# Two transformer blocks on one core: when groups are evicted, a stage's end barrier, the order of two loads and the place of a hosted sum

## The reference

```
mod = silu(c) @ w_mod + b_mod                     # shift, scale, gate rows
p   = modulate(rmsnorm(x), sh1, sc1) @ w_in       # mq mk mv mo mg | dq dk dv
h   = mlstm(forward) + flip(mlstm(backward))
y   = concat([rmsnorm(h) * sigmoid(mo), diff_heads]) @ w_out
x   = x + ga1 * rmsnorm(y, g_post_mix)
```

## Time and profile before

| | |
|---|---|
| time, median of 3 runs | 2983.63 us (2981.06 to 2983.66) |
| profiled execution | 2983.62 us, its span 2981.8 us |
| mean TensorE clock | 0.989 of full |
| busy TensorE / VectorE / ScalarE / GpSimd | 2867.1 / 2049.0 / 1243.8 / 145.2 us |
| HBM read | 572.21 MB |

### The profile page before, as it was taken

How to read it: one execution, slowest core, us unless ns; L and a number is a source line. 1 busy time by engine, 2 the same in 40 slices (tenths; PEclk the granted TensorE clock), 3 DMA queues, 4 the chain that set the end, 5 groups by cost and what they waited for, 6 DMA issues and landing times.

```text
span 2981.8 us, 38127 instructions
## 1 busy us (share of the span) xinstructions
PE 2867.1 (96%) x14307; PEld 2344.2 (79%) x14307; DVE 2049.0 (69%) x2919; ACT 1243.8 (42%) x2120; POOL 145.2 (5%) x225
## 2 busy tenths in 40 slices
PE   6999999998999999999999999999999999999998
PEld 2587667988778888887887888887878887888886
DVE  3368745837778889997895848873457686775466
ACT  3322525517345455454344332324445224445353
POOL 1100000001010000000000100000001001001000
PEclk9999999999999999999999999999999999999999
DMA  9877044841768777787886545772214564775334
GB/s 364 306 267 241 25 136 154 279 168 36 274 203 266 253 255 251 250 265 250 283 289 206 184 131 167 239 228 69 75 57 153 204 212 130 239 267 156 105 126 146
DMA packets 282822, 589.44 MB, mean 198 GB/s; under 512 B 31073, under 2 KB 64073, under 8 KB 278928
## 3 DMA queue, kind: packets, MB, share of 16 engines
q1 hardware_dynamic: 272240, 546.64, 56.0%
q0 software_dynamic: 10000, 39.72, 3.8%
q10 hardware_dynamic: 400, 0.66, 0.1%
HBM read 572.21 MB, written 14.72 MB: 197 GB/s over the span
## 4 chain that ended last, share of the span: by engine, by line
PE 75%; DVE 7%; ACT 3%; issue 2%; DMA 1%; POOL 0%; DVEq 0%; ACTq 0%; POOLq 0%
PE bank L3299 19%; PE bank L3301 19%; PE bank L3300 19%; PE bank L3309 2%; PE bank L3311 2%; PE bank L3310 2%; PE bank L1423 2%; DVE acc L739 2%; DVE w_lo L3236 1%; PE bank L1414 1%; ACT w_hi L3206 1%; PE bank L2453 1%; PE bank L883 1%; PE bank L1126 0%; PE bank L999 0%
## 5 line engine op out<-in xcount | busy, mean ns | idle before, releaser
L3236 DVE TENSOR_TENSOR w_lo<-raw,w_hi 128x1024 fp32r<-128x1024 f32 (+2 forms) x668 | 785.4, 1187 | 435.5 <-ACT w_hi L3206 428.0
L3206 ACT ACTIVATE w_hi<-raw 128x1024 fp32r<-128x1024 f32 (+2 forms) x668 | 679.6, 1031 | 913.9 <-PE bank L3301 639.1
L739 DVE SCALAR_TENSOR_TENSOR acc<-raw,sc_t,acc 128x1024 f32<-128x1024 f32 x480 | 601.3, 1280 | 23.6 <-DMA acc<-in_b_ada 18.7
L3299 PE MATMUL bank<-w_hi,l_hT_hi 128*128 128x512 f32 (+1 forms) x1056 | 390.2, 370 | 7.0 <-DVE w_lo L3236 4.8
L3301 PE MATMUL bank<-w_hi,l_hT_lo 128*128 128x512 f32 (+1 forms) x1056 | 387.6, 367 | 0.0
L3300 PE MATMUL bank<-w_lo,l_hT_hi 128*128 128x512 f32 (+1 forms) x1056 | 387.4, 367 | 0.0
L3299 PE MATMUL bank<-w_hi,f_hT_hi 128*128 128x512 f32 x704 | 278.1, 395 | 1.4 <-DVE mod L787 1.1
L3301 PE MATMUL bank<-w_hi,f_hT_lo 128*128 128x512 f32 x704 | 275.0, 391 | 0.0
L3300 PE MATMUL bank<-w_lo,f_hT_hi 128*128 128x512 f32 x704 | 274.8, 390 | 0.0
L3299 PEld LDWEIGHTS bank<-w_hi,l_hT_hi 128*128 128x128 f32 x1056 | 198.8, 188 | 43.7 <-DVE w_lo L3236 6.8
L3301 PEld LDWEIGHTS bank<-w_hi,l_hT_lo 128*128 128x128 f32 x1056 | 198.9, 188 | 31.5
(11 more groups left out here) (480 smaller groups left out, 4618.6 us busy)
## 6 DMA issues: line engine op xcount, KB each, us to landing
raw<-in_w_in SPq DMA_DIRECT2D x240, 512.0 KB, 4.8
raw<-in_w_mod SPq DMA_DIRECT2D x192, 512.0 KB, 5.3
raw<-in_w_ada SPq DMA_DIRECT2D x192, 512.0 KB, 4.5
raw<-in_w_up SPq DMA_DIRECT2D x176, 512.0 KB, 4.7
raw<-in_w_out SPq DMA_DIRECT2D x96, 512.0 KB, 4.9
raw<-in_w_down SPq DMA_DIRECT2D x88, 512.0 KB, 5.4
raw<-in_w_in SPq DMA_DIRECT2D x32, 288.0 KB, 3.2
raw<-in_w_ukv SPq DMA_DIRECT2D x32, 256.0 KB, 3.3
```

The lines of the kernel that those rows point to most:

```text
L739: e.scalar_tensor_tensor(acc[a][:, :], raw[s % RAW_SLOTS][:, :], scalar, acc[a][:, :], ALU.mult, ALU.add).then_inc(fma_done, 1)
L3206: e.activation(slot(w_hi[u % SPLIT_SLOTS], g.width), slot(raw[s % RAW_SLOTS], g.width), ACT.Copy).then_inc(hi_ready, 1)
L3236: e.tensor_tensor(slot(w_lo[u % SPLIT_SLOTS], g.width), slot(raw[s % RAW_SLOTS], g.width), slot(w_hi[u % SPLIT_SLOTS], g.width).bitcast(F3 ...
L3299: e.matmul(o, xh[:, k, tok], hi[:, kk, :], start=first, stop=False)
```

## The change

Three edits in block 1 and one in block 2's first layer:

1. In block 1's input projection mg leaves two units after its last one (it was one step), and the seven groups after it leave three units after their last (it was five steps). `later_hooks` uses the same count.
2. The recurrent stage has `runs_on`: no barrier at its end. The first two pieces of the output product's turn stand inside the stage's last pipeline step, in the written lists of TensorE, ScalarE and VectorE, and use banks 7 and 2. The other pieces follow one unit later than before on TensorE (q - 1; the pieces that wait for nothing of the recurrence at unit 1), their halves at step 0 for pieces 2 and 3. TensorE waits for the chain's last `dpart` before piece 2. `mix_pre` waits for a semaphore that ScalarE raises at its squares' end, stands at step 1, loops over heads first and reports after every second head; each recurrent piece waits for its own report. GpSimd waits for the stage's last a before it goes on. The group count is rounded up to an even number.
3. `residual_load` issues the gate row ahead of the residual.
4. Layer 0's second sum goes from (26, 17) to (24, 18), its third from (45, 14) to (47, 13).

```diff
@@ -245,6 +245,7 @@
         acc_ready = [sem(f"acc_ready{i}") for i in range(2)]
         sum_out = sem("sum_out")
+        m_squares = sem("m_squares")
         sum_rows = sem("sum_rows")
         sum_rows_copied = sem("sum_rows_copied")
@@ -350,12 +351,12 @@
         stage_count = [0]
-        def stage(early=None, ready=None, fill=0, joined=False, **engines):
+        def stage(early=None, ready=None, fill=0, joined=False, runs_on=False, **engines):
             stage_count[0] += 1
-            program.append(("stage", (early, ready, fill, joined), engines))
+            program.append(("stage", (early, ready, fill, joined, runs_on), engines))
         counted = {"main": 0, "slot": 0, "unit": 0, "fma": 0, "sum": 0, "group": 0, "mod": 0, "plain": 0, "rows": 0}
@@ -979,24 +980,28 @@
             return pe, act, dve
-        def turn_join(group0, X, tiles, hi, lo, order, held=0, more=None):
+        def turn_join(group0, X, tiles, hi, lo, order, held=0, more=None, first=0, spots=()):
             base = n_seen.setdefault("cat", 0)
...
             b0 = 4 - 4 * (counted["main"] % 2)
             w = P * nt
+            at_bank = [spots[i % len(spots)] if i < 2 * first else b0 + i % 4 for i in range(KT)]
             def turn_pe(q):
                 def pe(e):
                     if held and order[q] < held:
-                        e.wait_ge(mix_done, 1)
+                        e.wait_ge(mix_done, order[q] + 1)
+                    if first and q == first:
+                        e.wait_ge(m_dve_d, NCH)
                     for i in (2 * q, 2 * q + 1):
                         k = 2 * order[q] + i % 2
-                        if i >= 4:
-                            e.wait_ge(cat_lo_done, base + i - 3)
+                        users = [m for m in range(i) if at_bank[m] == at_bank[i]]
+                        if users:
+                            e.wait_ge(cat_lo_done, base + users[-1] + 1)
                         for t in range(nt):
-                            mm = e.transpose(banks[b0 + i % 4][:, P * t:P * t + P], X[:, t, P * k:P * k + P], ident)
+                            mm = e.transpose(banks[at_bank[i]][:, P * t:P * t + P], X[:, t, P * k:P * k + P], ident)
                         mm.then_inc(cat_tr, 1)
                 return pe
@@ -1004,7 +1009,7 @@
                     for i in (2 * q, 2 * q + 1):
                         e.wait_ge(cat_tr, base + i + 1)
-                        e.activation(hi[:, 2 * order[q] + i % 2, 0:w], banks[b0 + i % 4][:, 0:w], ACT.Copy).then_inc(cat_hi_done, 1)
+                        e.activation(hi[:, 2 * order[q] + i % 2, 0:w], banks[at_bank[i]][:, 0:w], ACT.Copy).then_inc(cat_hi_done, 1)
                 return act
@@ -1012,15 +1017,16 @@
                         k = 2 * order[q] + i % 2
                         e.wait_ge(cat_hi_done, base + i + 1)
-                        e.tensor_tensor(lo[:, k, 0:w], banks[b0 + i % 4][:, 0:w], hi[:, k, 0:w].bitcast(F32),
+                        e.tensor_tensor(lo[:, k, 0:w], banks[at_bank[i]][:, 0:w], hi[:, k, 0:w].bitcast(F32),
                                         ALU.subtract).then_inc(cat_lo_done, 1)
                 return dve
...
             def hooks(steps):
                 def parts(at):
-                    for q in range(KT // 2):
-                        yield "pe", at(group0, max(q - 2, 0)), turn_pe(q)
-                        later = at(group0, 7) + 1 if q == 7 else at(group0, q + 1)
+                    for q in range(first, KT // 2):
+                        ready_at = max(q - 2, 0) if not first else 1 if q < held else q - 1
+                        yield "pe", at(group0, ready_at), turn_pe(q)
+                        later = at(group0, 7) + 1 if q == 7 else 0 if q < held and first else at(group0, q + 1)
                         yield "act", later, hi_act(q)
                         yield "dve", later, lo_dve(q)
@@ -1033,6 +1039,8 @@
                 e.wait_ge(cat_tr, base + KT)
+            if first:
+                return hooks, ready, turned, dict(pe=turn_pe, act=hi_act, dve=lo_dve)
             return hooks, ready, turned
@@ -1866,10 +1874,12 @@
             return Group("A", w_in, KT, 3072 + 512 * q, 512, LAT_TILES, lhs1, a, d_)
-        mg.leave_after = 1
+        mg.leave_units = 2
         mk0, mo0, mk1, mo1 = mk_group(0), mo_group(0), mk_group(1), mo_group(1)
         mq0, mq1 = mq_groups()
         mv0, mv1 = mv_copy(0), mv_copy(1)
+        for g in (mk0, mo0, mk1, mo1, mq0, mq1, mv0):
+            g.leave_units = 3
@@ -2060,7 +2070,7 @@
             for at, g, j in mains:
                 if j == g.n_units - 1:
-                    leave = min(at + LEAVE_AFTER, len(steps))
+                    leave = leave_step(steps, at, g)
                     units = [at_ for at_, _, _ in mains if at_ > leave]
                     for who, behind, what in g.later:
@@ -2169,8 +2179,12 @@
             for s in range(-2, NCH + 1):
+                if s == NCH:
+                    mixed["pe"](0)(e)
                 if 0 <= s - 1:
                     c(s - 1)
+                if s == NCH:
+                    mixed["pe"](1)(e)
                 if 0 <= s < NCH:
                     b(s)
@@ -2223,8 +2237,12 @@
                 if s in (3, 5, 7, 9):
                     fill["act"](e, (s - 3) // 2)
+                if s == NCH:
+                    mixed["act"](0)(e)
                 if 0 <= s - 1 < NCH:
                     c(s - 1)
+                if s == NCH:
+                    mixed["act"](1)(e)
                 if s + 1 < NCH:
                     a(s + 1)
@@ -2232,6 +2250,7 @@
                 if 0 <= s - 2 and s % 2:
                     squares(s - 2)
+            e.sem_inc(m_squares, 1)
         def m_pool(e):
@@ -2288,6 +2307,9 @@
                 if s + 1 < NCH:
                     a(s + 1)
+                if s == NCH:
+                    mixed["dve"](0)(e)
+                    mixed["dve"](1)(e)
                 if 0 <= s - 1:
                     dpart(s - 1)
@@ -2295,7 +2317,7 @@
                     gained(s // 8)
-        stage(fill=SPLIT_SLOTS, pe=m_pe, act=m_act, pool=m_pool, dve=m_dve)
+        stage(fill=SPLIT_SLOTS, runs_on=True, pe=m_pe, act=m_act, pool=m_pool, dve=m_dve)
@@ -2304,14 +2326,16 @@
             n = 2 * HEADS
             y = tiny[:, n:2 * n]
+            e.wait_ge(m_squares, 1)
             rsqrt(e, tiny[:, 0:n], y, tiny[:, 2 * n:3 * n], 1.0 / HD)
-            for t in range(2):
-                for h in range(HEADS):
-                    c = slice(HD * h, HD * h + HD)
+            for h in range(HEADS):
+                c = slice(HD * h, HD * h + HD)
+                for t in range(2):
                     last = e.scalar_tensor_tensor(o1[:, t, c], o1[:, t, c], y[:, HEADS * t + h:HEADS * t + h + 1],
                                                   mo[:, t, c], ALU.mult, ALU.mult)
-            last.then_inc(mix_done, 1)
+                if h % 2:
+                    last.then_inc(mix_done, 1)
@@ -2319,8 +2343,8 @@
             def pool(e):
+                gate_load(gate, row, 1, stored)(e)
                 aux_dmas(e, [(X[:, 0:2, :], x_src.rearrange("(t p) d -> p t d", p=P))])
-                gate_load(gate, row, 1, stored)(e)
             return pool, need
@@ -2392,17 +2416,20 @@
         gs_out = [gated_group(A["w_out"][0], KT, q, (cat_hi, cat_lo), y1, gate1, 1) for q in range(4)]
         diff_first = [4, 5, 6, 7, 0, 1, 2, 3]
+        counted["main"] += counted["main"] % 2
         for g in gs_out:
             g.order = diff_first
...
         def mix(at):
-            yield "dve", at(gs_out[0], 2), mix_pre
+            yield "pool", 0, lambda e: e.wait_ge(m_a, NCH)
+            yield "dve", 1, mix_pre
             yield "pool", at(gs_out[0], 7) + 1, turned0
             yield "pool", at(gs_out[0], 7) + 1, res1
-        join0, ready0, turned0 = turn_join(gs_out[0], o1, LAT_TILES, cat_hi, cat_lo, diff_first, held=4, more=mix)
+        join0, ready0, turned0, mixed = turn_join(gs_out[0], o1, LAT_TILES, cat_hi, cat_lo, diff_first, held=4, more=mix,
+                                                  first=2, spots=(7, 2))
         res1, need1 = residual_load(X1, x_dram, gate1, 0, rows_mix)
         sums_ffn[3].late = True
@@ -2784,7 +2811,7 @@
             gemms(gs, sums_g0 + sums_l1[0] if not last else sums_g1, then=gates_stored,
-                  hosts=None if last else [(5, 15), (26, 17), (45, 14), (63, 12)],
+                  hosts=None if last else [(5, 15), (24, 18), (47, 13), (63, 12)],
                   hooks=in_hooks, ready=ready_norm, prev=prev, fill=3, late=late)
@@ -3137,7 +3164,7 @@
                     pending = True
                 else:
-                    early, ready, ahead, joined = how
+                    early, ready, ahead, joined, runs_on = how
                     if pending and not joined:
                         n_bar += 1
@@ -3154,8 +3181,9 @@
                     if who in what:
                         what[who](e)
-                    n_bar += 1
```

(4 more changed lines are left out.)

## The result

The changed kernel takes 2962.11 us, median of four runs (2960.71 to 2964.21); the kernel before takes 2983.64 on the same chip. The ratio is 0.9926, 95% interval 0.9914 to 0.9937. The forecast was 2963.1. The profiled execution took 2961.32 us.

What follows compares the result with a forecast made beforehand. TensorE, busy 96% of the span, bounds the kernel; only idle and half-clock time can be won. 4.9 + 4.85 + 4.8 + 6.0 = 20.55 off 2983.62 gives 2963.1 us; range 2957 to 2972, 8 in 10.

Steps and rivals of the forecast that it cites:

- Part 1: Block 1's input projection: evictions counted in weight units remove TensorE's waits at mk0, mo1 and mq1; 4.9 us.
- The estimate for unit 37: mk1 to mo1: ScalarE cuts unit 37 earlier, so it starts 1.7 us sooner; bounds 0 and 2.90.
- No clock is returned: At mk0's first unit: the 2.88 us wait goes, but no half-clock time is won, since none is lost there.
- Part 2: Recurrent stage's end: without the barrier, unit 4 of the output product starts earlier; 4.85 us, bounds 1 and 7.3.
- Part 3: Output product: gate row loaded first removes TensorE's 3.14 us wait and 1.65 of half clock; 4.8 us.
- Part 4: Layer 0: later third hosted sum removes waits of 3.86 and 0.70 and 1.65 of clock, less 0.2; 6.0 us.
- The seed's cover: Layer 0, unit 64: the fourth sum's seed comes 5.4 us later, using up its whole cover; costs 0.0 to 0.2.
- A: Output product: the burst still holds weights back, so the gate-first order wins nothing; 2967.9 us, chance 0.14.
- B: Recurrent stage's end: VectorE's list decides, unit 4 near 759.5, the hand-off gains only 1; 2966.9 us, chance 0.10.
- C: Layer 0, unit 64: the fourth sum's seed is late, 4.2 us of wait; 2967.3 us, chance 0.07.
- D: The waits go but two half-clock stretches stay, adding 3.3 us; 2966.4 us, chance 0.07.
- E: Feed-forward on: the even group count makes some 68 groups wait 0.8 us for evictions; 3017 us, chance 0.03.

Runs made afterwards that it cites:

- without part 1: Changed kernel with evictions in block 1's input projection counted in steps again, as in the kernel before: 2968.72 us, ratio 0.9945.
- four banks: Changed kernel with last two multiply parts, block 1's squares and residual load later, and early pieces in four banks, not two: 2961.72 us, ratio 0.9925.
- Part 2 alone: Kernel before with only the recurrent stage's end barrier removed and its new hand-off, residual still ahead of the gate row: 2982.78 us, ratio 0.9991.
- residual later: Changed kernel with the residual's 2 MB loaded only once unit 24 of the output product is through: 2963.19 us, ratio 0.9925.
- parity alone: Kernel before with only the group count rounded up to even ahead of the output product: 2983.07 us, ratio 0.9995.

## Why the prediction was right, point by point

The total came right because its four terms did, each to within 0.8, and not by luck of the rest: outside the four places the two traces differ by -1.4 ahead of mk0, 0.6 up to the stage's end, 0.9 near 850 and 0.8 behind unit 64, which add up to 0.9 us.

- **Part 1**, forecast 4.9. By the table mk0 to mq1 win 4.24 + 1.43 = 5.7. The estimate for unit 37 was good: 1.7 were forecast, the idle rows give 2.90 - 1.66 = 1.24, and the table 3.72 - 1.61 = 2.1. The rest is that a wait costs more than its idle row: the first matmul behind it takes 0.50 and not 0.39. "No clock is returned" was the execution's luck, as the kernel without part 1 showed.
- **Part 2**, forecast 4.85 with unit 4 15.2 us behind the stage's last matmul; it stands 15.4 behind it (750.82 - 735.42), where it stood 20.4: 5.0 won. VectorE's chain ran as written: the last step ended 4.2 behind (forecast 4.1), the multiplies began 9.5 (9.2) and ended 13.8 (13.5). The wait of 0.85 at unit 4 is for the low half behind the cut. The wait of 0.95 ahead of the second early piece was not forecast; it cost 0.4, as the kernel with four banks shows.
- **Part 3**, forecast 4.8: from unit 4 to 11 the table gives 12.67 - 9.83 = 2.84, and unit 12 comes 13.84 sooner, once the half clock behind the old wait has passed: 4.0. What is missing from 4.8 is the turned piece that moved behind unit 4 (0.4) and the new wait of 0.37. That VectorE would wait for matmuls only was wrong by 0.63.
- What the sum left out is that a faster hand-off meets the next load sooner. Parts 2 and 3 were forecast at 9.65 together; from the stage's end to unit 12 they gave 9.0 in the changed kernel's first trace and 7.9 in its second, in which the weights are waited for longer. Part 2 alone keeps 3.0 of its 5.0.
- **Part 4**, forecast 6.0: 3.86 and 0.70 went with the half clock, for which matching gives 4.0, 1.0 and 1.6. From unit 12 on it is 21.52 - 13.84 = 7.7, of which 0.9 (by matching again) came near 850, where a half-clock stretch stands in both traces and met other work. The seed's cover was used up to the tenth: the fourth sum's first row stands at 1935.60 (forecast 1957.25, less the 21.5 won by then), VectorE's cut of unit 64 ended at 1941.81 (1940.59 + 1.22), and TensorE took it at 1941.95.
- **Rivals.** A's mechanism is there at a tenth to a third of its price (residual later). B fell: unit 4 is where the forecast had it. C fell by 0.14 us of margin. D fell in this execution, all three windows being at full clock, though other stretches come and go. E fell (parity alone).

## What to carry to other kernels

Follow a hand-off to the next thing that the sped-up engine will ask for, and book its gain there and not at the hand-off: here 5.0 us at unit 4 were 3 to 4 at unit 12. Undo each edit in turn, and also do it alone, before two terms are called one; a second trace of the same kernel shows how far the rows spread. A wait for a load can be cured by its place in the queue; the load put behind it still slows the loads of the other queue, so move what nobody needs yet out of the burst.

## What the runs showed of the hardware that was not expected

- The same wait, 2.88 us for the same instruction, was followed by a half-clock stretch of 3.3 us in one kernel's execution and by none in another's; such a stretch cost 1.6 us when matched matmul by matmul (without part 1). Two stretches more or less, 3.2 us, make a difference as large as one of these edits.
- 2 MB behind a 1 MB load in GpSimd's queue did not slow that load (7.6 us with it and 7.9 without), and slowed SyncE's 0.5 MB loads beside it from 6.9 to 11.7 us (changed kernel, and residual later).
